# Seven-product pairs in the second down-projection of layers one to three of a streaming encoder

## The reference

```
def swiglu_ffn(x, w_in, w_out):
    g, u = jnp.split(x @ w_in, 2, axis=-1)
    return (jax.nn.silu(g) * u) @ w_out
xp = xp + swiglu_ffn(rmsnorm(xp, ffn_norms[i]), *ffn_params[i])
```

## Time and profile before

| | |
|---|---|
| median of 3 runs | 2535.23 us (2534.95 to 2535.63) |
| profiled execution | 2535.75 us, span 2533.5 us |
| PE busy | 2515.2 us, 99% of the span, 19925 matmuls |
| DVE busy | 1748.0 us, 69% |
| ACT busy | 1206.0 us, 48% |
| POOL busy | 166.5 us, 7% |
| granted TensorE clock | 0.999 of full speed |

### The profile page before, as it was taken

How to read it: one execution, slowest core, us unless ns; L and a number is a source line. 1 busy time by engine, 2 the same in 40 slices (tenths; PEclk the granted TensorE clock), 3 DMA queues, 4 the chain that set the end, 5 groups by cost and what they waited for, 6 DMA issues and landing times.

```text
span 2533.5 us, 48131 instructions
## 1 busy us (share of the span) xinstructions
PE 2515.2 (99%) x19925; PEld 2451.7 (97%) x19925; DVE 1748.0 (69%) x2579; ACT 1206.0 (48%) x1823; POOL 166.5 (7%) x180
## 2 busy tenths in 40 slices
PE   8999999999999999999999999999999999999998
PEld 8999999999988899999998899999999999999998
DVE  6555994984555599489557557948955565984973
ACT  5454651543555465245245545524534544642543
POOL 2101000001000010000122110000011101000001
PEclk9999999999999999999999999999999999999999
DMA  4222333332433233333222233332322223333332
GB/s 120 71 78 84 100 102 91 101 97 78 120 97 108 75 108 97 97 94 96 86 67 74 72 92 90 103 100 85 97 81 86 72 70 90 110 89 93 105 90 78
DMA packets 443890, 230.68 MB, mean 91 GB/s; under 512 B 17092, under 2 KB 440736, under 8 KB 443696
## 3 DMA queue, kind: packets, MB, share of 16 engines
q1 hardware_dynamic: 442048, 226.90, 31.2%
q10 hardware_dynamic: 1200, 0.59, 0.1%
q0 software_dynamic: 448, 0.45, 0.1%
HBM read 219.03 MB, written 8.87 MB: 90 GB/s over the span
## 4 chain that ended last, share of the span: by engine, by line
PE 95%; DVE 2%; issue 2%; ACT 0%; DMA 0%; POOL 0%; SPq 0%; DVEq 0%; ACTq 0%; POOLq 0%
PE slot L2388 32%; PE slot L2431 21%; PE aux L2900 6%; PE aux L2895 6%; PE aux L2897 6%; PE slot L2900 5%; PE slot L2895 5%; PE slot L2897 5%; PE aux L2347 2%; PE aux L2793 1%; PE aux L2556 1%; PE aux L2799 1%; PE aux L2705 1%; PE aux L2643 1%; PE aux L2571 1%
## 5 line engine op out<-in xcount | busy, mean ns | idle before, releaser
L765 ACT ACTIVATE w_hi<-raw 128x1024 fp32r<-128x1024 f32 (+3 forms) x207 | 239.5, 1157 | 270.1 <-PE slot L2431 136.7
L2388 PE MATMUL slot<-xg_hi,w_hi 128*128 128x272 f32 x1664 | 361.1, 298 | 2.9 <-DVE w_lo L1466 2.9
L2388 PE MATMUL slot<-xg_hi,w_lo 128*128 128x272 f32 x1664 | 343.9, 288 | 0.0
L2388 PE MATMUL slot<-xg_lo,w_hi 128*128 128x272 f32 x1664 | 343.8, 288 | 0.0
L1466 DVE TENSOR_TENSOR w_lo<-raw,w_hi 128x1024 fp32r<-128x1024 f32 (+4 forms) x207 | 282.5, 1365 | 67.1 <-ACT w_hi L765 65.1
L2388 PEld LDWEIGHTS slot<-xg_hi,w_hi 128*128 128x128 f32 x1664 | 260.8, 189 | 13.8 <-issue 6.9
L2388 PEld LDWEIGHTS slot<-xg_lo,w_hi 128*128 128x128 f32 x1664 | 261.4, 188 | 0.0
L2388 PEld LDWEIGHTS slot<-xg_hi,w_lo 128*128 128x128 f32 x1664 | 260.5, 189 | 0.0
L2107 DVE TENSOR_TENSOR ffn_y<-slot,rstd 128x544 f32<-128x544 f32 x56 | 40.6, 725 | 193.9 <-PE slot L2431 177.7
L2997 POOL TENSOR_TENSOR sq_sum<-sq_sum,sq_x 128x544 f32<-128x544 f32 x48 | 67.9, 1415 | 1608.4 <-ACT sq_x L783 1608.1
L2431 PE MATMUL slot<-h_hi,w_hi 128*128 128x272 f32 x1078 | 150.0, 287 | 0.0
(11 more groups left out here) (409 smaller groups left out, 5758.4 us busy)
## 6 DMA issues: line engine op xcount, KB each, us to landing
raw<-in_l_ffn_w_out_dram SPq DMA_DIRECT2D x64, 704.0 KB, 4.6
...
```

Of the source, the lines that this page charges most:

```text
L765: act.activation(w_hi[par][:, 0:kt, :], raw[par][:, 0:kt, :], ACT.Copy).then_inc(s_hi, 1)
L2388: ins = pe.matmul((slot[par] if bank is None else bank)[:, hf, 0:HALF], w[par][:, k, :], a[:, k0 + k, hf * HALF:(hf + 1) * HALF], start=(k ...
```

## The change

In down1 of layers one to three, output blocks 3 and 4 and output blocks 5 and 6 are each made as a seven-product pair over the first eight of the 11 k-tiles, and the other three k-tiles (`KX`) are added plainly into the same four PSUM sums (`rest_of`). The second column of those three weight tiles is negated, and that output is subtracted from `x`. Blocks 0, 1, 2 and 7 stay plain. The pairs use the two PSUM slots. The sums of quarters of `h` are made in the stage itself: POOL adds high and low parts of eight `h` tiles back to whole values (`whole_h`), DVE forms the sums (`h_sum`) and their low parts (`h_sum_low`), ACT their high parts (`t_half`). The buffers lie over those of the up stage's `t`. SP's loads, and the orders of ACT and DVE in this stage, are written anew (`project_seven` on each engine). Two semaphores of the GLA mixer are merged into one; the order of its instructions stays.

The diff, cut to its core (first constants and SP, then ACT, DVE, PE, POOL; `w_sums`, `lo_sums`, `hi_sums` and the like are those of the up stages):

```diff
+DOWN_PAIRS = (3, 5)
+KX = FH - XT
...
+            pair = aux if hf != "down" and u % 2 == 0 and (hf or u) else slot
             return pair[p0], pair[1 - p0]
...
+            if hf == "down":
+                return base[i, "down1"] + DOWN_PAIRS[u]
...
-                        down_load(m2)
+                    if hf == 0 or i == last:
+                        with sp.Fori(1, XT // 2) as m2:
+                            down_load(m2)
...
+                    def pair_load(j):
...
+                        here, there = (s_rawb, s_rawb) if s_buf[at] == "B" else (s_raw[p1], s_raw[1 - p1])
+                        sp.dma_start(into[:, first:first + KQ, :], wo_tiles(0, KQ, m + 1)).then_inc(here, 16)
+                        sp.dma_start(into[:, rest:rest + KQ, :], wo_tiles(KQ, XT, m + 1)).then_inc(there, 16)
+                        sp.dma_start(into[:, rest + KQ:rest + 3 * KQ, :], wo_tiles(0, XT, m)).then_inc(there, 16)
+                    def extra_load(j):
+                        p1, m = pair_at(i, "down", j) % 2, DOWN_PAIRS[j]
+                        sp.dma_start(extra_raw(p1).rearrange("p k a n -> p k (a n)"), wo_tiles(XT, FH, m, 2)).then_inc(s_raw[p1], 16)
+                    sp.wait_ge(s_lo, b0)
...
+                    load(b0 + 2, b0 % 2, wo_tiles(0, FH, 2), FH)
+                    sp.wait_ge(s_lo, b0 + 2)
+                    extra_load(0)
+                    sp.wait_ge(s_lo, b0 + 4)
+                    pair_load(1)
+                    sp.wait_ge(s_ws, 3 * s_no[i, "down", 1] + 1)
+                    extra_load(1)
+                    load(b0 + 7, (b0 + 7) % 2, wo_tiles(0, FH, XT - 1), FH, free=(s_lo, b0 + 7))
             y_rows = o[0].rearrange("a (t p) n -> (a p) t n", p=P)
             sp.wait_ge(s_yd, 1)
...
+                act.wait_ge(s_tdve, T_DVE * i + 16 + H_SUM_AT[q] + 3)
+                act.activation(one4(FF["t_hi"], q), one4(FF["hs"], q), ACT.Copy).then_inc(s_tact, 1)
...
+            def project_seven(i, b0):
+                p0 = b0 % 2
+                b3 = b0 + DOWN_PAIRS[0]
...
+                def x_ready(m):
+                    act.wait_ge(s_xd, XT * (2 * i + 1) + m + 1)
+                    x_square(norm_no(i, "down1"), m, m % 2, first=(m == 0))
+                    xg_split(m, norm_after(i, "down1"))
+                split(b0 + 1, 1 - p0, FH)
+                t_half(i, 0)
+                t_half(i, 1)
+                split(b0 + 2, p0, FH)
+                x_ready(0)
+                t_half(i, 2)
+                t_half(i, 3)
+                hi_sums(one_at, b3, None)
+                hi_more_sums(one_at, b3, None)
+                hi_extra(one_at, b3)
+                x_ready(1)
+                hi_a11(one_at, b3, None)
+                hi_rest(one_at, b3)
+                x_ready(2)
+                copy_product(one_at, b3 % 2, "d")
+                copy_product(one_at, b3 % 2, "b")
+                hi_sums(two_at, b3 + 2, "S")
+                hi_a11(two_at, b3 + 2, "S")
+                hi_more_sums(two_at, b3 + 2, "S")
+                hi_rest(two_at, b3 + 2)
+                hi_extra(two_at, b3 + 2)
+                copy_product(two_at, b3 % 2, "d")
+                copy_product(two_at, b3 % 2, "b")
+                x_ready(3)
+                x_ready(4)
+                split(b0 + 7, 1 - p0, FH)
+                split(b0 + 8, p0, next_k(i, "down1"))
...
+            def hi_extra(at, b):
...
+                if second:
+                    act.wait_ge(s_mm, b)
+                act.activation(extra(xg_hi)[:, 0, :, :], extra_raw(p1)[:, :, 0, :], ACT.Copy)
+                act.activation(extra(xg_hi)[:, 1, :, :], extra_raw(p1)[:, :, 1, :], ACT.Copy, scale=-1.0).then_inc(s_hi, 1)
...
+            def lo_extra(at, b):
...
+                dve.wait_ge(s_hi, b + 2 if at[2] else b + 1)
+                dve.tensor_tensor(extra(xg_lo)[:, 0, :, :], extra_raw(p1)[:, :, 0, :], extra(xg_hi)[:, 0, :, :].bitcast(F32),
+                                  ALU.subtract)
+                dve.scalar_tensor_tensor(extra(xg_lo)[:, 1, :, :], extra_raw(p1)[:, :, 1, :], -1.0,
+                                         extra(xg_hi)[:, 1, :, :].bitcast(F32), ALU.mult, ALU.subtract).then_inc(s_lo, 1)
...
+            def down_middle(at, b):
+                n, cd = s_no[at], up_banks(at[1], at[2], b % 2)[0]
+                dve.wait_ge(s_pr, 4 * n + 4)
+                dve.wait_ge(s_out7, 5 * n + 2)
+                dve.wait_ge(s_xd, XT * (2 * at[0] + 1) + DOWN_PAIRS[at[2]])
+                dve.tensor_tensor(FF["y"][:, 1:3, :], cd[:, :, 0:HALF], down_u2[:, :].unsqueeze(1).broadcast_to([P, 2, HALF]),
+                                  ALU.add).then_inc(s_free, 1)
+                dve.tensor_tensor(down_v[:, :], down_v[:, :], down_u2[:, :], ALU.add).then_inc(s_out7, 1)
+                dve.wait_ge(s_free, b + 1)
+                dve.tensor_tensor(FF["y"][:, 1, :], FF["y"][:, 1, :], rstd[:, HALF:TOK], ALU.mult)
...
+            def down_ends(at, b):
+                n, ab = s_no[at], up_banks(at[1], at[2], b % 2)[1]
+                dve.wait_ge(s_mm, b + 2)
+                dve.wait_ge(s_out7, 5 * n + 3)
+                dve.tensor_tensor(FF["y"][:, 3, :], ab[:, 1, 0:HALF], down_v[:, :], ALU.add).then_inc(s_out7, 1)
+                dve.tensor_tensor(FF["y"][:, 0, :], ab[:, 0, 0:HALF], rstd[:, 0:HALF], ALU.mult).then_inc(s_free, 1)
+                dve.wait_ge(s_out7, 5 * n + 4)
+                dve.tensor_tensor(FF["y"][:, 2:4, :], FF["y"][:, 2:4, :], halves(rstd[:, :]), ALU.mult).then_inc(s_out7, 1)
...
+            def h_sum(i, q):
...
+                dve.wait_ge(s_hx, XT * i + 2 * q + 2)
+                dve.tensor_tensor(tq[:, 0:2, :], hq[:, 0:4:3, :], hq[:, 1:2, :].broadcast_to([P, 2, HALF]),
+                                  ALU.subtract).then_inc(s_tdve, 1)
+                dve.wait_ge(s_tdve, at + 1)
+                dve.scalar_tensor_tensor(tq[:, 2, :], hq[:, 3, :], -1.0, tq[:, 0, :], ALU.mult, ALU.subtract).then_inc(s_tdve, 1)
+                dve.wait_ge(s_tdve, at + 2)
+                dve.scalar_tensor_tensor(tq[:, 3, :], tq[:, 2, :], -1.0, hq[:, 2, :], ALU.mult, ALU.subtract).then_inc(s_tdve, 1)
...
+            def h_sum_low(i, q):
+                dve.wait_ge(s_tact, T_ACT * i + 8 + q + 1)
+                dve.tensor_tensor(one4(FF["t_lo"], q), one4(FF["hs"], q), one4(FF["t_hi"], q).bitcast(F32),
+                                  ALU.subtract).then_inc(s_tdve, 1)
...
+            def project_seven(i, b0):
+                p0, norm = b0 % 2, norm_after(i, "down1")
+                b3 = b0 + DOWN_PAIRS[0]
...
+                def add(m, b):
+                    dve.wait_ge(s_mm, b + 1)
+                    if m:
+                        dve.wait_ge(s_xd, XT * (2 * i + 1) + m)
+                    dve.tensor_tensor(FF["y"][:, 0:2, :], slot[b % 2][:, :, 0:HALF], halves(rstd[:, :]), ALU.mult).then_inc(s_free, 1)
+                    dve.wait_ge(s_free, b + 1)
+                    dve.tensor_tensor(one(x, m), FF["g"], one(x, m), ALU.add).then_inc(s_xd, 1)
...
+                def low(m):
+                    xg_split(m, norm, m + split_tiles(i, "down1"))
...
+                split(b0 + 1, 1 - p0, FH)
+                h_sum(i, 0)
+                h_sum(i, 1)
+                h_sum_low(i, 0)
+                add(0, b0)
+                split(b0 + 2, p0, FH)
+                h_sum(i, 2)
+                low(0)
+                h_sum_low(i, 1)
+                h_sum(i, 3)
+                h_sum_low(i, 2)
+                w_sums(one_at, b3)
+                h_sum_low(i, 3)
+                add(1, b0 + 1)
+                lo_sums(one_at, b3)
+                lo_more_sums(one_at, b3, 2)
+                lo_extra(one_at, b3)
+                low(1)
+                add(2, b0 + 2)
+                lo_a11(one_at, b3, 3)
+                lo_rest(one_at, b3)
+                low(2)
+                c_plus_d(one_at, b3 % 2)
+                a_plus_b(one_at, b3 % 2)
+                w_sums(two_at, b3 + 2)
+                lo_sums(two_at, b3 + 2)
+                lo_a11(two_at, b3 + 2, 2)
+                lo_more_sums(two_at, b3 + 2, 3)
+                down_middle(one_at, b3)
+                down_ends(one_at, b3)
+                lo_rest(two_at, b3 + 2)
+                lo_extra(two_at, b3 + 2)
+                down_adds(one_at, b3)
+                c_plus_d(two_at, b3 % 2)
+                low(3)
+                low(4)
+                a_plus_b(two_at, b3 % 2)
+                split(b0 + 7, 1 - p0, FH)
+                down_middle(two_at, b3 + 2)
+                down_ends(two_at, b3 + 2)
+                down_adds(two_at, b3 + 2)
+                split(b0 + 8, p0, next_k(i, "down1"))
+                low(5)
+                low(6)
+                add(7, b0 + 7)
+                last_square(norm_no(i, "down1"))
+                low(7)
...
+            def seven_of_down(i, j):
...
+                def rest_of(to, which, half, start):
+                    hi, lo = of_h(XT, half)
```

(103 more changed lines are left out.)

82 lines of the change are left out of this document (56 added, 26 removed).

## The result

The kernel after takes **2557.82 us** (median of 4 runs, 2557.22 to 2558.62), the kernel before 2535.23 (2534.95 to 2535.63). The ratio is 1.0089, 95% interval [1.0076, 1.0101]: slower by 0.9%. Forecast were 2557.7 and +0.9%. The profiled execution took 2558.62 with a span of 2556.9; before these were 2535.75 and 2533.5.

A forecast was written before the change was run, and what follows sets the result against it. PE, busy 99% of the span, was taken as the bound. Waits of 10.5 us less 2.98 saved made each layer 7.5 us longer, three layers 22.5, giving 2557.7 us (+0.9%); range 2533 to 2566.

The forecast's parts named there:

- the walk: Layer one's down1 followed instruction by instruction at trace prices: waits of 10.5 us less 2.98 saved, 7.5 us longer a layer.
- hold on lines 2208, 2213, 2221, 2230 of before: End of the last `h` tile on DVE: these instructions wait 0.5, 1.2, 1.1 and 0.4 us beside POOL's additions.
- gap before block 2: PE waits 1.2 us for the high part of block 2's weights, which ACT makes after its sums' high parts.
- scale of block 1: DVE instruction freeing the slot that pair one writes, forecast to end at 587.6 while PE finished block 2 at 583.5.
- gap before pair one: PE waits 4.15 us for DVE's scale of block 1, behind DVE's gapless run of new work.
- scale of block 2: DVE instruction inside pair one, at 593.3 to 594.1, needed by the third product: PE waits 2.55 us.
- gaps inside pair one: PE waits 0.9 us for `lo_sums`, 2.55 for the scale of block 2, 1.7 for `c_plus_d`.
- The step that carried the sum: Two-SBUF-input instructions on DVE and POOL's additions alternate; the second waits for the first, about 1.2 us for DVE.
- DVE is not held: Rival: POOL waits and DVE never does; 2.4 us of waits a layer against 2.98 saved, 2533.5 us; chance 0.12.
- the whole gain: Rival: DVE's work before pair one fits and the later waits are shorter; 8.95 us saved, 2526.3 us; chance 0.11.
- milder hold: Rival: DVE's blocks as computed, but gaps elsewhere absorb half of the extra 8 us; 2545 us; chance 0.12.
- The clock did fall: Rival: after its waits PE runs pair one's first 60 matmuls at 1.2 GHz, +2.3 us a layer, 2565; chance 0.07.

The follow-up runs named there:

- e2: Kernel after with 30 extra matmuls on PE ahead of pair one's first wait, into a bank nobody reads then: 2557.79 us, ratio 1.0087.
- e1: Kernel after with POOL's eight additions of `h` replaced by constant fills, which write but read nothing: 2540.48 us, ratio 1.002.
- e3: Kernel after with the eight additions of `h` on DVE, two ahead of each `h_sum`, none on POOL: 2557.94 us, ratio 1.0089.
- e5: Kernel after with POOL copying the high part of `h` instead of adding high and low parts: 2543.33 us, ratio 1.0032.
- e6: Kernel after with each of POOL's eight additions made twice, sixteen in a row: 2582.25 us, ratio 1.0186.

## Why the prediction was right

Point by point, layer one, each interval or time as forecast and as measured (the stage began 0.43 us earlier than the walk had it, which is taken off the forecast times):

| step | forecast | measured |
|---|---|---|
| matmuls fewer, us a layer | 24, 2.98 | 24 |
| hold on lines 2208, 2213, 2221, 2230 of before | 0.5, 1.2, 1.1, 0.4 | 0.70, 1.17, 0.98, 0.36 |
| gap before block 2 | 1.2 | 1.0 (574.77 less 565.54 + 8.20) |
| scale of block 1 ends | 587.2 | 587.14 |
| gap before pair one | 4.15 | 4.2 |
| scale of block 2 starts | 592.9 | 592.88 |
| `c_plus_d` ends | 598.3 | 598.23 |
| gaps inside pair one | 0.9, 2.55, 1.7 | 0.8, 0.9, none at the lower clock; in e2 0.8, 2.6, 1.5 |
| waits in pair two and block 7 | none | none |
| stage longer by | 7.5 | 8.23 |

The step that carried the sum, that POOL's additions and DVE's two-operand instructions take turns, was read in the forecast from six rows of another stage; e1, e3, e5 and e6 show it by taking it away, moving it, shortening it and doubling it. The rival "DVE is not held" falls with the rows of 1.88 and 2.52 us, "the whole gain" with the 3.94 us wait. The "milder hold" falls too: DVE had no gap after 564.39 that could have absorbed anything.

What was off:
- **The clock did fall**, which the forecast gave 0.07. PE idled for 4 us, and the granted clock went to 1.2 GHz in all three layers (0.50 in the window above). The rival's mechanism happened; its price was wrong. It had the slow matmuls outlast the later waits by 2.3 us a layer. The slow stretch was shorter, nearly 40 matmuls in place of 60, at 0.226 us in place of 0.25 (back at full speed by 599 in layer one, by about 1251 in layer two), and it lay over exactly the waits that the forecast had as 2.55 and 1.7: in layer one only 0.65 of the first is left and nothing of the second. Against e2, which is 7.65 us longer than before in layer one where 7.5 was forecast, the fall costs 0.58 us: PE reached the fifth product at 598.99, with `c_plus_d` done at 598.23. This is most of the 0.7 between 7.5 and 8.23. Without the clock the walk was right within 0.2 us, its gaps 0.4 too long in all, while the slow first group behind each wait, which it left out, took 0.5. The Trainium skill, "TensorE: Matmul & The Clock Gate", section "Part 1: The HAM clock gate (the "warmup" mystery)", has a PE left idle go back to half rate; the trace agrees (1.2 GHz behind the wait of 3.94 us).
- **Without POOL's reads the change is still slower** (e1, 2540.5), where the case "DVE is not held" had 2533.5. That sum had 2.4 us of waits a layer, and e1 shows 3.97 and the restarts. It held DVE nowhere, by its own premise, while in e1 the additions of squares still hold L2282 (which frees the third product's slot later) and a low part ahead of `c_plus_d`. And the walk let PE start again at once: the scale ends at 588.88 in e1, PE starts at 589.03, and its first group takes 0.08 more. PE's starts on both sides of the 2.39 us wait are 3.05 apart (585.98 to 589.03), 2.55 more than 0.50.
- **That 2557.7 meets 2557.82 so closely is in part luck.** The stages are longer by 8.2, 7.6 and 8.2, 24.1 us in all, 1.6 more than the forecast's 22.5; the span is 23.4 longer and the medians 22.6. The rest of the program is 0.7 us shorter in the profiled execution: 0.43 of it ahead of the first down1, which begins anywhere from 557.3 to 558.3 us in the runs here, and 0.26 between the down1 of layer two and the down0 of layer three, the cause of which is open. The other 0.8 is that the profiled execution was the slowest of the four (2558.62, at a granted clock of 0.994 where the others had 0.996).
